# Output stage of a two-block kernel: three split weight buffers, a tile-by-tile end, and table loads behind the Silu

## The chip, the cores and the metric

The kernel runs as one program on one core of a Trainium2 chip. The metric is the device time of one execution in microseconds (us). Three runs of the kernel before gave 2280.24, 2282.44 and 2284.18 us, a median of 2282.44 us. The profile that is quoted below comes from another execution.

Engines carry the names of the profile: PE is TensorE (PEld its weight loads), DVE is VectorE, ACT is ScalarE, POOL is GpSimd, SP is SyncE, which here only issues DMAs.

## The reference

Two model blocks run one after the other over 512 tokens of width 1024, all in float32. The first is a gated mix of convolution and attention with a feed-forward part; the second holds an RWKV-7 mixer and then a latent attention (MLA) mixer. Only the end of the MLA mixer and what follows it is touched here:

```python
MLA_HEADS = 16; QK_NOPE = 128; QK_ROPE = 64; V_HEAD = 128      # D_INNER = 16 * 128 = 2048

def _rms_norm(x, g):
    y = xf * lax.rsqrt(jnp.mean(xf * xf, axis=-1, keepdims=True) + RMS_EPS)
    return (y * g).astype(x.dtype)

def _mla_mixer(x, pos, ...):
    h = x @ w_in                       # c_q, c_kv, k_rope and the gate input g
    ...
    o = _causal_block_attention(q_nope, q_rope, k_nope, k_rope, v).reshape(B, L, D_INNER)
    return (o * jax.nn.silu(g)) @ w_out            # [512, 2048] @ [2048, 1024]

h = h + _rms_norm(m, norm_post[i])
return h[:, N_META:]                   # the 16 meta tokens are dropped
```

## The kernel before

**Precision by three products.** A float32 product is made of three PE matmuls on parts rounded to a shorter format: high x high, high x low, low x high (`product`, L157 to L161). A weight block therefore has to be split before PE may use it: SP loads 512 KB or so into one of two `raw` buffers, and POOL writes the high part (L147) and then the low part (L150) into one of two buffers `w_hi`/`w_lo`. Such a block is a unit `u`; its buffers are those of slot `u % 2`. `split_ready` counts the splits, `unit_done` the units that PE has finished. POOL starts the split of unit `u` when unit `u - 2`, which used the same slot, is done.

**The head loop.** The 16 heads `h` run in the order written in the code, PE in `head_pe`, ACT in `head_act`, DVE in `head_dve`. A head has four query tiles `t`. For each tile PE computes scores, DVE takes the negative maximum `nmax`, ACT takes Exp (L2589), DVE normalises (reciprocal L2619, multiply L2622), PE transposes (`turn`, L2472 and L2474), DVE copies the result out (L2629, L2630), and after the four tiles PE makes the values product (L2489, L2491). DVE multiplies the result with the gate (L2605) and rounds it (`z2_hi`, L2607), POOL makes the low part (`z_low`, L2667). Between these steps PE does "fills" for the next heads, each written into a PSUM bank that must have been emptied first: `v0`, `v1`, `v2` (value weights, in even heads; banks 4, 5 and again 4), `rope` (in odd heads, bank 4), `gate` (bank 6), `ka`, `qn`, `kb` for the next head (banks 5, 4, 5). ACT empties the banks of all but the gate: `v_tok` (L2370, L2364), `q_sw` (L2356, four quarter copies), `kn_hi` (L2362), `qn_hi` (L2359). Head 13 has a shorter gate fill than the others; the rest of that gate is done in heads 13 and 14.

**Activation tables.** Exp and Silu are in different ACT tables. In heads 1 to 13 ACT does the Silu of gate `h + 1` right after the Exp of tile 1 (`gate_silu`, L2373 to L2376), and the Silu of gate 15 in head 14 just after the `ka` copy. The program gets an ACT_TABLE_LOAD ahead of the Silu (recorded at L2376) and one ahead of the next Exp (recorded at L2589).

**The output stage.** The 16 rows of blocks of `w_out`, `k` = 0 to 15, are the last 16 units. A "cell" is one token tile `t` (0 to 3) and one half of the 1024 output columns: three matmuls of 512 columns. A unit has eight cells, and all cells of the eight (tile, half) pairs accumulate in the eight PSUM banks (`OUT_BANK`). Unit 2 has a split buffer of its own, `out2_hi`/`out2_lo` (L2279 to L2287), which lies in memory that is free once gate 15 is done; units 0, 1 and 3 to 15 use the two slots. Units 0 and 1 and part of the stage's work are put into the last heads. POOL's order is: split 0, split 1, `z_low(14)`, split 2, `z_low(15)`, split 3 to 15. PE does units 2 to 13 with all cells, then unit 14 for tiles 0 and 1, then waits for unit 15's split and goes on tile by tile (L2566 to L2578).

**The end.** For each tile: ACT squares the 1024 columns and sums them (L2841), POOL adds epsilon (L2739) and takes the power -0.5 (L2741) into `fin_r`, DVE multiplies each half by `fin_r` and the norm weight `post_row` (L2936) and adds the residual `h_fin` (L2939), SP sends each half out (L2708).

Of the kernel before, what the change touches and what calls it, by code (L numbers as in the profile page):

```python
# [18 lines left out]
P = 128  # L19
# [51 lines left out]
def program(nc, io, out):  # L71
    with ExitStack() as base:
# [2058 lines left out]
        ssq, fin_r = put("ssq", [P, 2 * QB]), put("fin_r", [P, 2 * QB])  # L2131
# [147 lines left out]
        def split_out2(pool):  # L2279

            u = U_MO + 2
            pool.wait_ge(landed[u % 2], landings(u, u % 2))
            pool.wait_ge(unit_done, UNIT_AT["gate", MH - 1] + 1)
            nc.gpsimd.tensor_scalar(out2_hi[:], raw[u % 2][:, 0:D], 1.0, 0.0, ALU.mult, ALU.add).then_inc(split_hi, 1)
            pool.wait_ge(split_hi, u + 1)
            nc.gpsimd.tensor_tensor(out2_lo[:], raw[u % 2][:, 0:D], out2_hi[:].bitcast(F32), ALU.subtract).then_inc(split_ready, 1)
            pool.wait_ge(split_ready, u + 1)  # L2287
# [268 lines left out]
        def out_pe(pe):  # L2556
# [9 lines left out]
            for k in range(2, MH - 2):  # L2566
# [3 lines left out]
            pe.wait_ge(split_ready, U_MO + MH - 1)  # L2570
            pe.wait_ge(zl_ev, MH - 1)
# [98 lines left out]
        with nc.Block() as block:  # L2670
            @block.sync
            def _(sp):
# [30 lines left out]
                for k in range(2, MH):  # L2703
# [10 lines left out]
            def _(pool):  # L2714
# [259 lines left out]
```

## Time and profile before

| what | value |
|---|---|
| median of 3 runs | 2282.44 us (2280.24 to 2284.18) |
| the profiled execution's own time | 2284.97 us |
| its span | 2283.1 us |
| PE busy | 2235.6 us, 98% |
| DVE, ACT, POOL busy | 1237.7 us (54%), 831.5 us (36%), 1156.5 us (51%) |
| TensorE clock granted | 0.994 over the span |
| DMA queue of the program | 184.76 MB, 27.0% of 16 engines |

The profiled execution took 2.5 us more than the median; 1.9 us of its 2284.97 us lie outside its span. A line of the profile names the source line, the engine, the operation, the tiles written and read with partitions and elements, and how many were merged (x2). In brackets stands how long the engine sat idle before it and what released it. Matmul ends are modelled, so the distance between the starts of matmuls is the better measure of PE's pace.

### The profile page before, as it was taken

The numbers are of one execution on the slowest core, as the hardware profiler recorded it, in microseconds if no ns is written. First come the engines' busy times: TensorE is split into PE (matmuls) and PEld (weight loads), VectorE is DVE, ScalarE is ACT, GpSimd is POOL, SyncE is SP. The second block draws the span as 40 slices with busy tenths as digits, with TensorE's granted clock in tenths as the row PEclk, the third lists the DMA queues.
The fourth block names the chain that finished last, engine by engine and source line by source line (L and its number), as shares of the span: only waits on it lengthen the run. The fifth ranks groups of instructions, "written<-read, shape, count | busy, mean of one in ns | idle before, by whom it ended". The sixth has DMA issues, their size and how long they took to land.

```text
span 2283.1 us, 51404 instructions
## 1 busy us (share of the span) xinstructions
PE 2235.6 (98%) x21811; PEld 1805.1 (79%) x21811; DVE 1237.7 (54%) x2314; ACT 831.5 (36%) x1717; POOL 1156.5 (51%) x803
## 2 busy tenths in 40 slices
PE   8999999999999999999999999999998999999998
PEld 7778888788888677777777777777888878888876
DVE  4353357877831845555565566666531565555521
ACT  4122212333311445555555555554321343443300
POOL 4555567787765253444444444444546344343355
PEclk9999999999999999999999999999999999999999
DMA  3323323333332221222222222223323321221222
GB/s 115 83 75 84 83 87 92 95 97 97 104 102 97 71 63 60 69 80 83 73 69 78 69 69 69 71 75 128 130 66 106 106 74 47 58 63 42 76 96 92
DMA packets 262108, 188.04 MB, mean 82 GB/s; under 512 B 18283, under 2 KB 242409, under 8 KB 261497
## 3 DMA queue, kind: packets, MB, share of 16 engines
q1 hardware_dynamic: 261881, 184.76, 27.0%
q8 instruction: 174, 2.85, 0.5%
q14 instruction: 53, 0.43, 0.1%
HBM read 162.69 MB, written 22.04 MB: 81 GB/s over the span
## 4 chain that ended last, share of the span: by engine, by line
PE 90%; DVE 5%; POOL 2%; issue 1%; ACT 1%; SPq 0%; DMA 0%; POOLq 0%; DVEq 0%; ACTq 0%
PE ps L1353 19%; PE ps L159 16%; PE ps L160 15%; PE ps L161 15%; PE ps L1539 3%; PE ps L1555 3%; PE ps L1581 2%; PE ps L1528 2%; PE ps L1366 1%; PE ps L1495 1%; PE ps L2489 1%; PE ps L221 1%; PE ps L1467 1%; PE ps L1484 1%; PE ps L1517 1%
## 5 line engine op out<-in xcount | busy, mean ns | idle before, releaser
L150 POOL TENSOR_TENSOR w_lo<-raw,w_hi 128x1024 fp32r<-128x1024 f32 (+1 forms) x177 | 451.4, 2550 | 14.8
L147 POOL TENSOR_SCALAR w_hi<-raw 128x1024 fp32r<-128x1024 f32 (+1 forms) x177 | 195.4, 1104 | 480.6 <-PE ps L161 470.6
L159 PE MATMUL ps<-h_hi,w_hi 128*128 128x512 f32 x616 | 243.1, 395 | 1.8 <-DVE h_lo L1062 1.7
L161 PE MATMUL ps<-h_hi,w_lo 128*128 128x512 f32 x616 | 240.1, 390 | 0.0
L160 PE MATMUL ps<-h_lo,w_hi 128*128 128x512 f32 x616 | 239.7, 389 | 0.0
L1353 PE MATMUL ps<-mixed_k,raw 128*64 128x264 f32 x1024 | 149.3, 387 | 0.0
L1353 PE MATMUL ps<-mixed_r,raw 128*64 128x264 f32 x1024 | 143.9, 387 | 0.0
L1353 PE MATMUL ps<-mixed_g,raw 128*64 128x264 f32 x1024 | 138.2, 386 | 0.0
L159 PEld LDWEIGHTS ps<-h_hi,w_hi 128*128 128x128 f32 x616 | 115.8, 188 | 26.1 <-DVE h_lo L1062 2.8
L161 PEld LDWEIGHTS ps<-h_hi,w_lo 128*128 128x128 f32 x616 | 115.6, 188 | 24.4
L160 PEld LDWEIGHTS ps<-h_lo,w_hi 128*128 128x128 f32 x616 | 115.8, 188 | 23.2
L1353 PE MATMUL ps<-mixed_v,raw 128*64 128x264 f32 x1024 | 129.2, 389 | 2.4 <-DMA raw<-in_rwkv_w_in_dram 2.4
L1077 DVE SCALAR_TENSOR_TENSOR up_c<-up_raw,params,up_c 128x512 f32<-128x512 f32 x88 | 119.1, 1358 | 20.3 <-ACT up_c L832 18.7
L1881 DVE TENSOR_TENSOR x_m<-ps,lv_pad 128x640 f32<-128x640 f32 (+2 forms) x160 | 110.9, 726 | 9.7 <-PE ps L1539 5.2
L1945 POOL TENSOR_TENSOR kp<-k_b,kp 128x528 f32<-128x528 f32 x16 | 29.6, 1849 | 169.3 <-ACT kp L1674 169.3
L1539 PEld LDWEIGHTS ps<-t_m,mb 128*64 128x64 f32 x2752 | 96.1, 138 | 15.4 <-ACT mb L1662 3.4
L1353 PEld LDWEIGHTS ps<-mixed_v,raw 128*64 128x64 f32 x1024 | 69.6, 137 | 36.8 <-issue 5.4
L1539 PE MATMUL ps<-t_m,mb 128*64 128x64 f32 x2752 | 97.5, 222 | 0.2 <-DVE t_m L1887 0.2
L1962 POOL MEMSET uv<- 64x64 f32 x32 | 4.6, 145 | 178.8 <-PE ps L1510 177.9
L2589 ACT ACTIVATE xT<-ps,nmax 128x144 f32<-128x144 f32 (+1 forms) x64 | 34.4, 539 | 158.2 <-DVE nmax L2614 157.9
L1628 ACT ACTIVATE uv<-ps 64x64 f32<-64x64 f32 x128 | 27.9, 218 | 161.6 <-PE ps L1484 161.6
L1555 PEld LDWEIGHTS ps<-x_m,t_t 128*64 128x64 f32 x2240 | 77.8, 138 | 9.4 <-DVE x_m L1881 0.6
(462 smaller groups left out, 5959.3 us busy)
## 6 DMA issues: line engine op xcount, KB each, us to landing
raw<-in_rwkv_w_in_dram SPq DMA_DIRECT2D x64, 512.0 KB, 4.4
raw<-in_w_up_dram SPq DMA_DIRECT2D x44, 512.0 KB, 3.8
raw<-in_w_in_dram SPq DMA_DIRECT2D x41, 512.0 KB, 3.9
raw<-in_w_down_dram SPq DMA_DIRECT2D x22, 512.0 KB, 3.6
raw<-in_mla_w_in_dram SPq DMA_DIRECT2D x22, 512.0 KB, 4.0
sb_kept<-xT SPq DMA_DIRECT2D x16, 528.0 KB, 2.7
xT<-sb_kept SPq DMA_DIRECT2D x16, 528.0 KB, 4.7
raw<-in_rwkv_w_out_dram SPq DMA_DIRECT2D x16, 512.0 KB, 3.9
```

Source lines behind the costliest of these rows:

```text
L147: nc.gpsimd.tensor_scalar(w_hi[s][:, 0:width], raw[s][:, 0:width], 1.0, 0.0, ALU.mult, ALU.add).then_inc(split_hi, 1)
L150: nc.gpsimd.tensor_tensor(w_lo[s][:, 0:width], raw[s][:, 0:width], w_hi[s][:, 0:width].bitcast(F32), ALU.subtract).then_inc(split_ready, 1)
L159: nc.tensor.matmul(dst, w[0], x[0], start=start, stop=False)
L160: nc.tensor.matmul(dst, w[0], x[1], start=False, stop=False)
L161: return nc.tensor.matmul(dst, w[1], x[0], start=False, stop=stop)
L1077: nc.vector.scalar_tensor_tensor(out=up_c[:, ab, 1 + k, :], in0=up_raw[:, n % 4, 1 - k:1 - k + T1], scalar=prm(("cf1", "cf0")[k], n // 2 + ...
L1353: mm = nc.tensor.matmul(dst[m, :], raw_k[t % 2][:, k, m], mixed[t][:, k, cols], start=(k == 0), stop=(k == KD - 1))
L1528: mm = nc.tensor.matmul(ps[:, 2 + 3 * h + q, x * P:x * P + P], bk[own[h], c0 + x, :], rkv[own[h], c0 + x, 0:2 * C], start=True, stop=True)
L1539: mm = nc.tensor.matmul(ps[own[h], 2 + p, x * C:x * C + C], mb[:, c0 + x, own[h]], t_m[:, c0 + x, :], start=True, stop=True)
L1555: mm = nc.tensor.matmul(dst, t_t[:, c0 + x, :], x_m[:, c0 + x, h, :], start=True, stop=True)
L1581: mm = nc.tensor.matmul(ps[m, 6 + h, 0:T2 // 2], halves_ones[:, m], src(h), start=True, stop=True)
L1881: nc.vector.tensor_tensor(x_m[:, c0:c0 + m, :, :], part_of(2 + p, m).unsqueeze(2).to_broadcast([P, m, 2, C]), lv_pad[:, lv - 1, :, :].unsq ...
```

## The change

Five things are changed, all at the end of the second block.

1. **Three weight buffers.** Units 2, 5, 8, 11 and 14 of the output stage use the extra buffer, units 3, 6, 9, 12, 15 that of unit 0, units 4, 7, 10, 13 that of unit 1. The split of unit `k` (from 3 on) now waits until PE has finished unit `k - 3`, not `k - 2`. SP loads unit 2 ahead of `h_fin` and `post_row`.
2. **The split of unit 2** stands ahead of `z_low(14)` on POOL, where it stood behind it.
3. **Tile by tile.** PE does all cells only up to unit 12. Units 13 and 14 are done for tiles 0 and 1, then unit 15 for tile 0, then for tile 1; tiles 2 and 3 then get their cells of units 13, 14 and 15 one half after the other, with a signal after tile 2 and after each half of tile 3.
4. **The final norm.** DVE multiplies by `post_row` first, as soon as the square sum is there, and then does one operation with `fin_r` and `h_fin` per half. For tile 3 ACT squares the halves apart and takes the root itself by Ln and Exp(-0.5 x); POOL still adds epsilon to the first half's sum.
5. **Table loads.** After each Silu from gate 2 on, ACT loads the Exp table at once.

The diff, cut to its core:

```diff
+        def slot_of(u):
+            return u % 2
...
+        def out_buffer(k):
+            if k % 3 == 2:
+                return out2_hi, out2_lo
+            s = slot_of(U_MO + k % 3)
+            return w_hi[s][:, 0:D], w_lo[s][:, 0:D]
+        def split_out(pool, k):
+            u = U_MO + k
+            s, (hi, lo) = slot_of(u), out_buffer(k)
+            pool.wait_ge(landed[s], landings(u, s))
+            pool.wait_ge(unit_done, UNIT_AT["gate", MH - 1] + 1 if k == 2 else u - 2)
...
             act.wait_ge(gate_raw, g + 1)
             nc.scalar.activation(gate[:, g, :], gate[:, g, :], ACT.Silu).then_inc(gate_ev, 1)
+            if g > 1:
+                nc.scalar.preload_act_table_set(LOG_EXP)
...
-            for k in range(2, MH - 2):
+            for k in range(2, MH - 3):
                 pe.wait_ge(split_ready, U_MO + k + 1)
                 pe.wait_ge(zl_ev, k + 1)
                 out_cells(pe, k, ALL_CELLS).then_inc(unit_done, 1)
-            out_cells(pe, MH - 2, [(0, 0), (0, 1), (1, 0), (1, 1)])
+            for k in (MH - 3, MH - 2):
+                pe.wait_ge(split_ready, U_MO + k + 1)
+                pe.wait_ge(zl_ev, k + 1)
+                out_cells(pe, k, [(0, 0), (0, 1), (1, 0), (1, 1)])
             pe.wait_ge(split_ready, U_MO + MH)
             pe.wait_ge(zl_ev, MH)
-            for t in range(QB):
-                if t >= 2:
-                    out_cells(pe, MH - 2, [(t, 0), (t, 1)])
+            for t in range(2):
                 out_cells(pe, MH - 1, [(t, 0), (t, 1)]).then_inc(o_mm, 1)
+            for half in range(2):
+                for k in range(MH - 3, MH):
+                    mm = out_cells(pe, k, [(2, half)])
+            mm.then_inc(o_mm, 1)
+            for half in range(2):
+                for k in range(MH - 3, MH):
+                    mm = out_cells(pe, k, [(QB - 1, half)])
+                mm.then_inc(o_mm, 1)
...
                 for k in range(2):
                     load_out_rows(sp, k)
+                load_out_rows(sp, 2)
                 sp.wait_ge(unit_done, UNIT_AT["gate", MH - 1] + 1)
                 sp.wait_ge(s_h, 48)
                 sp.dma_start(h_fin[:], h_rows_kept).then_inc(s_h, 16)
                 sp.dma_start(post_row[:], io["norm_post_2"][1].partition_broadcast(P)).then_inc(s_h, 16)
-                for k in range(2, MH):
+                for k in range(3, MH):
                     load_out_rows(sp, k)
...
+                split_out(pool, 2)
                 z_low(pool, MH - 2)
-                split_out2(pool)
                 z_low(pool, MH - 1)
                 for k in range(3, MH):
-                    split_mla(pool, U_MO + k)
+                    split_out(pool, k)
...
+                t = QB - 1
+                for half in range(2):
+                    act.wait_ge(o_mm, QB + half)
+                    at = (t, 2 * QB)[half]
+                    nc.scalar.activation(squares[...512 columns...], ps[:, OUT_BANK[t] + half, :],
+                                         ACT.Square, scale=D ** -0.5, accum_out=ssq[:, at:at + 1]).then_inc(o_sq, 1)
+                act.wait_ge(o_eps, QB)
+                act.wait_ge(o_sq, QB + 1)
+                nc.scalar.activation(..., ACT.Ln, bias=ssq[:, QB + t:QB + t + 1]).then_inc(o_eps, 1)
+                act.wait_ge(o_eps, QB + 1)
+                nc.scalar.activation(fin_r[:, t:t + 1], ..., ACT.Exp, scale=-0.5).then_inc(o_r, 1)
...
                 for t in range(QB):
+                    for half in range(2):
+                        dve.wait_ge(o_sq, t + 1 + (half if t == QB - 1 else 0))
+                        nc.vector.tensor_tensor(o_tok[:, t, cols], ps[:, OUT_BANK[t] + half, :], post_row[:, cols],
+                                                ALU.mult).then_inc(o_step, 1)
                     dve.wait_ge(o_r, t + 1)
                     for half in range(2):
-                        nc.vector.scalar_tensor_tensor(out=o_tok[:, t, cols], in0=ps[:, OUT_BANK[t] + half, :], scalar=fin_r[:, t:t + 1],
-                                                       in1=post_row[:, cols], op0=ALU.mult, op1=ALU.mult).then_inc(o_step, 1)
                         dve.wait_ge(o_step, 2 * t + half + 1)
-                        nc.vector.tensor_tensor(o_tok[:, t, cols], o_tok[:, t, cols], h_fin[:, t, cols], ALU.add).then_inc(o_ev, 1)
+                        nc.vector.scalar_tensor_tensor(out=o_tok[:, t, cols], in0=o_tok[:, t, cols], scalar=fin_r[:, t:t + 1],
+                                                       in1=h_fin[:, t, cols], op0=ALU.mult, op1=ALU.add).then_inc(o_ev, 1)
```

The order of the instructions on ACT in an even head (head 12; the other even heads with a Silu, 2 to 10, read the same). Before, from the Silu (`gate`) over the copies of the value fills (`v_tok`) to the Exp of tile 2 (`xT` from 128x400):

```order
L2376 ACT_TABLE_LOAD
L2376 ACTIVATE gate<-gate 128x512 [waits gate_raw]
L2370 ACTIVATE v_tok<-ps 128x512 [waits oo_mm,up_mm]
L2370 ACTIVATE v_tok<-ps 128x512 [waits up_mm]
L2589 ACT_TABLE_LOAD [waits pt_mm]
L2589 ACTIVATE xT,psum_r<-ps,nmax 128x400 [waits sc_max]
```

And now:

```order
L2387 ACT_TABLE_LOAD
L2387 ACTIVATE gate<-gate 128x512 [waits gate_raw]
L2389 ACT_TABLE_LOAD
L2381 ACTIVATE v_tok<-ps 128x512 [waits oo_mm,up_mm]
L2381 ACTIVATE v_tok<-ps 128x512 [waits up_mm]
L2608 ACTIVATE xT,psum_r<-ps,nmax 128x400 [waits pt_mm,sc_max]
```

The second load moved from behind the two `v_tok` copies to ahead of them. The number of loads in the head is the same.

ACT in head 14 and at the start of head 15, where the Silu of gate 15 stands. Before:

```order
L2376 ACT_TABLE_LOAD
L2376 ACTIVATE gate<-gate 128x512 [waits gate_raw]
L2359 ACTIVATE qn_hi<-ps 128x512 [waits up_mm]
L2362 ACTIVATE kn_hi<-ps 128x264 [waits unit_done]
L2589 ACT_TABLE_LOAD [waits pt_mm]
L2589 ACTIVATE xT,psum_r<-ps,nmax 128x144 [waits sc_max]
```

And now:

```order
L2387 ACT_TABLE_LOAD
L2387 ACTIVATE gate<-gate 128x512 [waits gate_raw]
L2389 ACT_TABLE_LOAD
L2370 ACTIVATE qn_hi<-ps 128x512 [waits up_mm]
L2373 ACTIVATE kn_hi<-ps 128x264 [waits unit_done]
L2608 ACTIVATE xT,psum_r<-ps,nmax 128x144 [waits pt_mm,sc_max]
```

The load moved from ahead of head 15's first Exp to ahead of the copies `qn_hi` and `kn_hi` that head 15's scores are made of.

POOL around the split of unit 2 (`out_hi`, `out_lo`). Before:

```order
L147 TENSOR_SCALAR w_hi<-raw 128x1024 [waits unit_done,split_ready,landed1]
L150 TENSOR_TENSOR w_lo<-raw,w_hi 128x1024 [waits split_hi]
L2667 TENSOR_TENSOR z_lo<-xT,z_hi 128x512 [waits zh_ev,zt_ev,split_ready]
L2284 TENSOR_SCALAR out_hi<-raw 128x1024 [waits unit_done,landed0,zl_ev]
L2286 TENSOR_TENSOR out_lo<-raw,out_hi 128x1024 [waits split_hi]
L2667 TENSOR_TENSOR z_lo<-xT,z_hi 128x512 [waits zh_ev,zt_ev,split_ready]
```

And now:

```order
L150 TENSOR_SCALAR w_hi<-raw 128x1024 [waits unit_done,split_ready,landed1]
L153 TENSOR_TENSOR w_lo<-raw,w_hi 128x1024 [waits split_hi]
L2295 TENSOR_SCALAR out_hi<-raw 128x1024 [waits unit_done,landed0,split_ready]
L2297 TENSOR_TENSOR out_lo<-raw,out_hi 128x1024 [waits split_hi]
L2686 TENSOR_TENSOR z_lo<-xT,z_hi 128x512 [waits zh_ev,zt_ev,split_ready]
L2686 TENSOR_TENSOR z_lo<-xT,z_hi 128x512 [waits zh_ev,zt_ev,zl_ev]
```

The two operations of the split stand directly behind those of unit 1, and both `z_lo` operations behind them.

## Rows read from the trace of the kernel before

**Rows 1.** The page's chain that ended last, shares of the span by engine.

```profile
PE 90%; DVE 5%; POOL 2%; issue 1%; ACT 1%; SPq 0%; DMA 0%; POOLq 0%; DVEq 0%; ACTq 0%
```

**Rows 2.** Timeline of head 2: start, duration, engine, line, operation [idle before, releaser].

```profile
1901.68 0.63 ACT L2376 ACTIVATE gate<-gate 128x512 f32<-128x512 f32 x1
...
1902.22 1.07 ACT L2370 ACTIVATE v_tok<-ps 128x512 f32<-128x512 f32 x2
...
1902.69 0.23 PE L2452 MATMUL ps<-causal_b,ident_b 128*128 128x128 bf16 x1
...
1902.94 0.28 PE L159 MATMUL ps<-w_hi,ckv_hi 128*16 128x256 f32 x1
...
1903.30 1.28 ACT L2589 ACT_TABLE_LOAD   x1
```

**Rows 3.** Timeline of PE in head 0, the same place.

```profile
1859.60 0.23 PE L2452 MATMUL ps<-causal_b,ident_b 128*128 128x128 bf16 x1
1859.64 0.31 PE L159 MATMUL ps<-w_hi,ckv_hi 128*16 128x256 f32 x1
```

**Rows 4.** Timelines of ACT and PE in head 3.

```profile
1923.28 2.39 ACT L2356 ACTIVATE q_sw<-ps 32x512 f32<-32x512 f32 x4 [2.18 <-PE ps L161]
1925.69 1.28 ACT L2589 ACT_TABLE_LOAD   x1
1927.47 0.19 ACT L2589 ACTIVATION_READ_ACCUMULATOR xT<-ps,nmax 128x1 f32 x1
...
1927.46 0.31 PE L2474 MATMUL ps<-ident,xT 128*128 128x32 f32 x2
1927.72 0.39 PE L159 MATMUL ps<-kn_hi,qn_hi 128*128 128x264 f32 x1
```

**Rows 5.** Timeline of head 13, scores of tile 3 and the next low part.

```profile
2144.05 0.39 PE L159 MATMUL ps<-kn_hi,qn_hi 128*128 128x264 f32 x1 [1.33 <-ACT xT L2589]
...
2147.50 0.43 DVE L2395 TENSOR_TENSOR kn_lo<-ps,kn_hi 128x264 fp32r<-128x264 f32 x1 [0.60 <-ACT kn_hi L2362]
```

**Rows 6.** Timeline of head 14 behind the Silu of gate 15.

```profile
2169.47 0.58 ACT L2359 ACTIVATE qn_hi<-ps 128x512 fp32r<-128x512 f32 x1
...
2171.47 0.63 PE L2472 MATMUL ps<-ident,xT 128*128 128x128 f32 x4 [0.18 <-DVE xT L2630]
```

**Rows 7.** Timeline of heads 14 and 15 around the split of unit 2.

```profile
2171.45 2.37 POOL L150 TENSOR_TENSOR w_lo<-raw,w_hi 128x1024 fp32r<-128x1024 f32 x1
...
2176.84 0.43 DVE L2607 CAST z_hi<-xT 128x512 fp32r<-128x512 f32 x1
...
2179.99 2.55 DVE L2622 TENSOR_SCALAR xT<-xT,prec 128x272 f32<-128x272 f32 x1
2180.02 2.36 POOL L2286 TENSOR_TENSOR out_lo<-raw,out_hi 128x1024 fp32r<-128x1024 f32 x1
...
2182.60 0.44 PE L2472 MATMUL ps<-ident,xT 128*128 128x128 f32 x2 [1.90 <-DVE xT L2622]
```

**Rows 8.** DMA issues from 2120 us on: KB each, median us to landing.

```profile
raw<-in_mla_w_out_dram SPq DMA_DIRECT2D x16, 512.0 KB, 3.3
```

**Rows 9.** Timelines of POOL, PE, ACT and DVE at the end.

```profile
2261.91 1.05 POOL L147 TENSOR_SCALAR w_hi<-raw 128x1024 fp32r<-128x1024 f32 x1 [1.90 <-PE ps L161]
...
2265.47 0.50 PE L159 MATMUL ps<-w_hi,z_hi 128*128 128x512 f32 x1 [1.13 <-POOL w_lo L150]
...
2267.16 1.03 ACT L2841 ACTIVATE squares<-ps 128x1024 f32<-128x1024 f32 x1 [81.04 <-PE ps L161]
2268.08 0.19 ACT L2841 ACTIVATION_READ_ACCUMULATOR squares<-ps 128x1 f32 x1
...
2273.96 1.02 ACT L2841 ACTIVATE squares<-ps 128x1024 f32<-128x1024 f32 x1 [1.60 <-PE ps L161]
...
2269.44 0.75 DVE L2936 SCALAR_TENSOR_TENSOR o_tok<-ps,fin_r,post_row 128x512 f32<-128x512 f32 x1 [76.11 <-POOL fin_r L2741]
...
2279.94 0.69 DVE L2939 TENSOR_TENSOR o_tok<-o_tok,h_fin 128x512 f32<-128x512 f32 x1
```

More of the change, by code:

```diff
@@ L2130, in program @@
         nmax, psum_r, prec = put("nmax", [P, 2]), put("psum_r", [P, 2]), put("prec", [P, 2])
-        ssq, fin_r = put("ssq", [P, 2 * QB]), put("fin_r", [P, 2 * QB])
+        ssq, fin_r = put("ssq", [P, 2 * QB + 2]), put("fin_r", [P, 2 * QB])
         assert put.end <= 121, put.end
@@ L2277, in split_mla @@
             split_unit(pool, u, u % 2, width=1280 if wide else 1024)
[L2279 to L2284, printed above, removed]
+        def out_buffer(k):
[8 more added lines that the diff above has]
+            pool.wait_ge(unit_done, UNIT_AT["gate", MH - 1] + 1 if k == 2 else u - 2)
+            nc.gpsimd.tensor_scalar(hi[:], raw[s][:, 0:D], 1.0, 0.0, ALU.mult, ALU.add).then_inc(split_hi, 1)
             pool.wait_ge(split_hi, u + 1)
-            nc.gpsimd.tensor_tensor(out2_lo[:], raw[u % 2][:, 0:D], out2_hi[:].bitcast(F32), ALU.subtract).then_inc(split_ready, 1)
+            nc.gpsimd.tensor_tensor(lo[:], raw[s][:, 0:D], hi[:].bitcast(F32), ALU.subtract).then_inc(split_ready, 1)
             pool.wait_ge(split_ready, u + 1)
@@ L2495, in out_cells @@
         def out_cells(pe, k, cells):
-            s = (U_MO + k) % 2
+            hi, lo = out_buffer(k)
             for t, half in cells:
                 cols = slice(512 * half, 512 * half + 512)
-                w = (out2_hi[:, cols], out2_lo[:, cols]) if k == 2 else w_cols(s, 512 * half, 512)
                 mm = product(ps[:, OUT_BANK[t] + half, :], (z2_hi[:, k, P * t:P * t + P], z2_lo[:, k, P * t:P * t + P]),
-                             w, k == 0, k == MH - 1)
+                             (hi[:, cols], lo[:, cols]), k == 0, k == MH - 1)
             return mm
@@ L2739, in _ @@
                     nc.gpsimd.tensor_scalar(ssq[:, QB + t:QB + t + 1], ssq[:, t:t + 1], EPS, None, ALU.add).then_inc(o_eps, 1)
-                    pool.wait_ge(o_eps, t + 1)
-                    nc.gpsimd.tensor_tensor(fin_r[:, t:t + 1], ssq[:, QB + t:QB + t + 1], eps_col[:, 3:4], ALU.pow).then_inc(o_r, 1)
+                    if t < QB - 1:
+                        pool.wait_ge(o_eps, t + 1)
+                        nc.gpsimd.tensor_tensor(fin_r[:, t:t + 1], ssq[:, QB + t:QB + t + 1], eps_col[:, 3:4], ALU.pow).then_inc(o_r, 1)
             @block.tensor
@@ L2838, in _ @@
                     head_act(act, h)
-                for t in range(QB):
+                for t in range(QB - 1):
                     act.wait_ge(o_mm, t + 1)
@@ L2842, in _ @@
                                          ACT.Square, scale=D ** -0.5, accum_out=ssq[:, t:t + 1]).then_inc(o_sq, 1)
+                t = QB - 1
+                for half in range(2):
+                    act.wait_ge(o_mm, QB + half)
+                    at = (t, 2 * QB)[half]
+                    nc.scalar.activation(squares[:, t, 512 * half:512 * half + 512], ps[:, OUT_BANK[t] + half, :],
+                                         ACT.Square, scale=D ** -0.5, accum_out=ssq[:, at:at + 1]).then_inc(o_sq, 1)
+                act.wait_ge(o_eps, QB)
+                act.wait_ge(o_sq, QB + 1)
+                nc.scalar.activation(ssq[:, 2 * QB + 1:2 * QB + 2], ssq[:, 2 * QB:2 * QB + 1], ACT.Ln,
+                                     bias=ssq[:, QB + t:QB + t + 1]).then_inc(o_eps, 1)
+                act.wait_ge(o_eps, QB + 1)
+                nc.scalar.activation(fin_r[:, t:t + 1], ssq[:, 2 * QB + 1:2 * QB + 2], ACT.Exp, scale=-0.5).then_inc(o_r, 1)
             @block.vector
```

3 lines of the change are left out of this document (1 added, 2 removed).

## The prediction

> **What bounds the kernel now.** I read the page first: PE is busy 98% of the span, and 90% of the chain that ended last is PE [rows 1]. So until the last matmul a wait costs time only if PE waits for it, and a wait on PE costs its full length, since nothing behind it gives it back. Then the waits of PE and the timelines of the heads, one even and one odd head in full. The reader is to see there that PE hardly waits, but that in several places it goes on within 0.1 us of the end of an ACT or DVE operation. Such a place is tight: what delays that operation delays PE by the same amount. The end of the span is the exception: from the first `o_tok` operation at 2269.44 to the last at 2279.94 (its end 2280.63) the bound is DVE [rows 9].
>
> **Part 5, table loads, even heads with a Silu (2, 4, 6, 8, 10, 12).** In head 2 the Silu runs 1901.68 to 2.31, the copies of fills `v0` and `v1` start at 1902.22, overlapping its tail, and the table load follows at 1903.30 [rows 2]. PE's fill `v2` goes into the bank of `v0` and so waits for the first copy. PE issues it at 1902.94, 0.25 us behind the matmul before it, where in head 0, which has no Silu, the distance is 0.04 us [rows 3]. The first copy of 0.6 us ends at 1902.82, just ahead of 1902.94. So this place is tight, and the copy is what PE waits for. The change puts the load between Silu and copy: it can start at 1902.31 and takes 1.28 us (1.29 with its gap, as 1925.69 in [rows 4]), so the copy starts at 1903.61 and not 1902.22: 1.39 us later, and PE with it. The load that goes from behind the copies was hidden beside the gate fill. Six heads: 6 x 1.39 = **+8.3 us**. Bounds: 0, if the gap of 0.25 us is something else, and 8.3; I take 8.3, since rows 2 give the order of events to 0.1 us.
>
> The Trainium skill (ScalarE: Activation LUTs, "What ACT_TABLE_LOAD costs") counts about 2.66 us for each switch, a load of 1283 ns and a drain of 1380 ns. The rows agree with the first number and show no drain: the load starts 0.02 us behind the quarter copies' end at 2.39 us after 1923.28 [rows 4]. By the page's sum the even heads would lose some 16 us.
>
> **Odd heads.** There ACT is idle 2.18 us ahead of the four `q_sw` copies [rows 4], which covers a load of 1.29 us. The load it replaces stood between `q_sw` and the Exp of tile 2. That Exp ends at 1927.66, and PE starts the scores of tile 3 at 1927.72; PE's two matmuls before start at 1927.46 and are 0.31 us long together, so it could have gone on near 1927.58; with the shorter first step I take 0.14 us. Six heads (1, 3, ... 11): -0.8 us. In head 13 the gate fill in front is half as long and PE waits 1.33 us for the Exp [rows 5]. The load's 1.29 us go, but next the fill `kb` waits for DVE's `kn_lo` at 2147.50, which hangs on DVE's own queue (rope work) and moves by only 0.1 us; PE would reach it 0.15 us too early. Net **-1.1 us**. Odd heads together -1.9 us.
>
> **Head 14.** The Silu of gate 15 is followed by `qn_hi` at 2169.47; DVE's `qn_lo` and the copy of turn 2 come behind it in DVE's order, and PE's turn 3 at 2171.47 already waits 0.18 us for that copy [rows 6]. The load moves this chain by 1.39 us: **+1.4 us**. The load that goes stood ahead of head 15's first Exp; PE does not wait for that Exp directly, so nothing comes back.
>
> **Part 2, the split of unit 2.** In head 15 a DVE multiply of 128x272 takes 2.55 us: it starts 0.03 us before POOL's `out_lo` and ends 0.16 us behind it [rows 7]. PE's turn 1 waits 1.90 us for it. What the row shows is that DVE gets nothing done on two SBUF operands or in its fast form while such a POOL operation runs. The Trainium skill says the same (GPSIMD Reference, "Specifications": SBUF interfaces shared with VectorE, contention with instructions in a 2-port mode or with two SBUF inputs); it would have me expect the same stall wherever the split goes. The new place: unit 1's split ends at 2173.82 [rows 7], so unit 2's runs to about 2177.5. DVE has only PSUM reads there in the shifted head 14 (its rounding of `z2_hi`, at 2176.84 before, comes at 2178.2). The data must have landed by 2174: its load is issued at 2167.9 as before, takes 3.3 us [rows 8], and no longer queues behind `h_fin`. So **-1.9 us**. If `z2_hi` met the split, 0.4 us would come back.
>
> **Parts 1 and 3, PE at the end.** From the Square of tile 0 at 2267.16 to that of tile 3 at 2273.96 PE does 30 matmuls: 0.227 us each, 5.44 for a unit of 24 [rows 9]. Split 15 starts at 2261.91 when unit 13 is done, and PE waits 1.13 us for it at 2265.47. With three buffers it starts a unit earlier, at 2256.5, and the wait goes; with the slower restart I count 1.3 us. Matmuls number the same.
>
> **Parts 3 and 4, the tail.** Before: first Square at 2267.16, sum at 2268.27, POOL's epsilon and power, DVE at 2269.44, then 8 x (0.7 + 0.7) = 11.2 us of DVE. Now tile 0 is ready 14 cells (42 matmuls) before the end and not 10: its Square starts near 2263, tile 1's 2264.4, tile 2's 2268.5, the halves of tile 3 at 2270.6 and 2273.96 - 1.3 = 2272.7. DVE is then free of a backlog: per tile two multiplies and two final operations, about 0.6 to 0.7 each, 2.5 us, against tiles that come 4.1 and 2 us apart; tile 2 is done by 2272.2. The last half decides. Square of 512 columns: 1.11 us for 1024 [rows 9], so between 0.55 and 1.11, I take 0.77; sum at 2273.4; multiply from 2273.5, 0.6; Ln and Exp on one column lie beside it (two short ACT operations, bounded by the 0.19 of the accumulator read below and the 0.6 of a 512 copy above); two final operations, 1.4: DVE ends at 2275.5 (2275.2 to 2276.3). From DVE's end to the span's end is 2283.1 - 2280.63 = 2.47 us for the last store; the two last stores now come 0.7 us apart instead of 1.4, for which I leave 0.1. Span end 2278.0, that is **-5.1 us** with the 1.3 of PE in it (-4.3 to -5.4).
>
> **The sum.** +8.3 - 1.9 + 1.4 - 1.9 - 5.1 = +0.8 us on the profiled span of 2283.1, thus 2283.9. The median of the runs is 2282.44, so I predict 2283.2 us. The two sides are each about 9 us and nearly cancel.
>
> **The rivals.**
> - *The reload costs nothing in the even heads* (the gap of 0.25 us is not the copy, or PE makes the loss good later). For it: the page shows ACT busy only 36%, and the load is short. Against: rows 2 and 3, and PE without slack. Time: 2283.2 - 8.3 = 2274.9; half of it recovered gives 2279.
> - *The tail gives only PE's wait* (slower than before). Mechanism: DVE's final operation now reads `o_tok` and `h_fin`, both in SBUF, and waits for `fin_r`; if a POOL operation of the root or the new multiply in front pushes each tile past the next one, DVE stays the bound as before, with 11.2 us behind the first Square's successor. It decides if a tile's DVE work is over 4.1 us (I count 2.5). Then -5.1 becomes about -1.3, and the time 2287.0. Against: the old second operation also had two SBUF operands and took 0.69 [rows 9].
> - *The change does not do what it says in part 2*: the split meets DVE's rounding and `z_low` then sits in front of the first multiply; the 1.9 us come back, 2285.1.
> - *A switch of tables waits for a drain*. As a mechanism of this kernel: ACT would be held behind each load for as long again as the load lasts, which in six even heads and head 14 adds 7 x 1.3 = 9 us: 2292. Rows 4 speak against it. The Trainium skill's section named above has that rule; by the trace it does not hold.
>
> **How the numbers follow.** My sum 64%; reload free or largely made good 15%; tail only PE's wait 6%; part 2 void 12%; drain 3%. My sum's own error is about 1.5 us, and three runs spread over 4 us. The range 2278.0 to 2287.0 takes in my sum, part 2 void and the half-recovered case, and leaves out most of the first rival and the drain. This kernel tells a difference from none at about 0.2%, 4.6 us: faster is under 2277.9, slower above 2287.0. Faster: 15% x 0.8 and a rest of the sum's error, 0.14. Slower: 3% + half of 6% and a rest, 0.08. Same: 0.78.
>
> **What would show it.** Head 2 of the changed kernel: the first `v_tok` copy 1.4 us behind where it was, and PE idle about 1.4 us before the `v2` fill, six times. PE's wait in head 13 gone, the one before turn 3 of head 14 grown from 0.18 to 1.6. The 128x272 multiply of head 15 down to well under 1 us and PE's 1.90 us wait gone. No wait of PE for a split in the output stage; last matmul to span end 5.5 us, where it was 9. A PE that does not wait for `v0` in the even heads would make the prediction wrong by up to 8 us.

## The result, and the profile after

The changed kernel is slower. Median of 20 runs 2286.34 us (2283.94 to 2288.60); 20 runs of the kernel before beside them gave 2282.07 us. The ratio is 1.002 with a 95% interval of 1.0014 to 1.0026, so 3 to 6 us slower. Predicted were 2283.2 us, within 2278.0 to 2287.0, and no measurable difference. The time lies inside the range, but 3.5 us of it were not in my sum, and most of this part of the document is about them.

The two profiled executions hardly differ (span 2283.2 us now, 2283.1 before; own time 2284.88 and 2284.97). Read by that alone, the change costs nothing. The page shows the same picture as [rows 1], with DVE's share of the chain down from 5% to 4%:

```profile
PE 90%; DVE 4%; POOL 2%; ACT 2%; issue 1%; SPq 0%; DMA 0%; DVEq 0%; POOLq 0%; ACTq 0%
```

A profile of the whole is a poor ruler here, because the part ahead of the heads, which is the same code in all kernels, took 1857.3 to 1861.5 us in the 14 profiles I have. So I cut every profile in three: the front, up to the start of the Exp of tile 2 in head 0; the heads, from there to the start of the last Exp of head 15; the tail, to the end of the span.

| profile | front | heads | tail |
|---|---|---|---|
| before | 1860.5 | 324.9 | 97.8 |
| after | 1858.2 | 332.5 | 92.5 |
| after - before | -2.3 | +7.6 | -5.3 |

The front's -2.3 us does not come from the change: before had one more stretch at half TensorE clock there, in the same code. The touched parts cost +2.3 us, not 0.

**Even heads.** Timeline of head 2 after the change; it answers to [rows 2].

```profile
1899.27 0.63 ACT L2387 ACTIVATE gate<-gate 128x512 f32<-128x512 f32 x1
...
1899.92 1.28 ACT L2389 ACT_TABLE_LOAD   x1
...
1900.28 0.23 PE L2465 MATMUL ps<-causal_b,ident_b 128*128 128x128 bf16 x1
...
1901.22 1.09 ACT L2381 ACTIVATE v_tok<-ps 128x512 f32<-128x512 f32 x2
...
1901.96 0.28 PE L162 MATMUL ps<-w_hi,ckv_hi 128*16 128x256 f32 x1 [1.45 <-ACT v_tok L2381]
```

The load sits between Silu and `v_tok`; the copy begins 0.02 us behind it; PE stands idle for 1.45 us until the copy of `v0` has emptied the bank. The waits of PE over the heads (line waited for, us in total, times, longest):

```profile
PE ps L162 <- ACT v_tok L2381: 8.7, 6, 1.5
PE ps L2485 <- DVE xT L2641: 2.7, 7, 0.4
PE ps L2485 <- DVE xT L2649: 1.8, 2, 1.6
PE ps L162 <- DVE kn_lo L2408: 0.2, 1, 0.2
```

Six times 1.45 us for the copy, and no wait for it before. From tile 2 to tile 3 each of these heads is 1.37 to 1.42 us longer than before, except head 10 with 2.97.

**Head 10.** PE's timeline across its wait, then the same stretch by windows (us, busy time and count of PE, PEld, DVE, ACT and POOL, then granted clock, DMA share, GB/s).

```profile
2078.39 0.23 PE L2465 MATMUL ps<-causal_b,ident_b 128*128 128x128 bf16 x1
2080.07 0.28 PE L162 MATMUL ps<-w_hi,ckv_hi 128*16 128x256 f32 x1 [1.45 <-ACT v_tok L2381]
...
2081.20 0.63 PE L162 MATMUL ps<-u_hi,w_hi 128*128 128x512 f32 x1
2081.63 0.63 PE L163 MATMUL ps<-u_lo,w_hi 128*128 128x512 f32 x1
2082.06 0.63 PE L164 MATMUL ps<-u_hi,w_lo 128*128 128x512 f32 x1
...
2083.72 0.39 PE L162 MATMUL ps<-u_hi,w_hi 128*128 128x512 f32 x1
```

```profile
1960.00:2078.00 118.00, 113.82 (x674) 96.23 (x674) 68.84 (x162) 47.02 (x94) 50.37 (x29) 1.00 0.23 61
2078.00:2086.00 8.00, 6.55 (x30) 5.12 (x30) 1.34 (x5) 3.34 (x7) 0.17 (x1) 0.79 0.00 0
```

Before its wait PE runs at the full clock (2.4 GHz, 1.00 in the first window). Right behind the end of the wait it falls to the half (1.2 GHz): matmuls of 512 columns then start 0.43 us apart, and from 2083.72 on 0.23 us apart again. The clock record of this core has this stretch at 2080.2 us, 3.4 us long. It costs 2.97 - 1.40 = 1.6 us. The kernel before has a granted clock of 1.00 throughout the heads.

**Head 14**, answering to [rows 6]:

```profile
2175.61 1.28 ACT L2389 ACT_TABLE_LOAD   x1
...
2176.91 0.60 ACT L2370 ACTIVATE qn_hi<-ps 128x512 fp32r<-128x512 f32 x1
...
2178.93 0.63 PE L2485 MATMUL ps<-ident,xT 128*128 128x128 f32 x4 [1.59 <-DVE xT L2649]
```

PE's wait ahead of turn 3 has grown from 0.18 to 1.59 us.

**Split of unit 2**, answering to [rows 7]: both POOL operations end before DVE comes to them.

```profile
2177.49 2.35 POOL L153 TENSOR_TENSOR w_lo<-raw,w_hi 128x1024 fp32r<-128x1024 f32 x1
...
2181.07 2.35 POOL L2297 TENSOR_TENSOR out_lo<-raw,out_hi 128x1024 fp32r<-128x1024 f32 x1
...
2184.30 0.43 DVE L2626 CAST z_hi<-xT 128x512 fp32r<-128x512 f32 x1
...
2187.45 0.36 DVE L2641 TENSOR_SCALAR xT<-xT,prec 128x272 f32<-128x272 f32 x1
```

**The tail**, answering to [rows 9]. The halves of tile 3, Ln and Exp on ACT, the last matmul, and DVE's last two operations:

```profile
2275.86 0.60 ACT L2868 ACTIVATE squares<-ps 128x512 f32<-128x512 f32 x1 [0.93 <-PE ps L164]
...
2277.47 0.39 PE L164 MATMUL ps<-w_hi,z_lo 128*128 128x512 f32 x1
...
2277.90 0.60 ACT L2868 ACTIVATE squares<-ps 128x512 f32<-128x512 f32 x1 [1.35 <-PE ps L164]
...
2278.68 0.29 ACT L2872 ACTIVATE ssq<-ssq 128x1 f32<-128x1 f32 x1
2279.00 0.20 ACT L2875 ACTIVATE fin_r<-ssq 128x1 f32<-128x1 f32 x1
2279.24 1.41 DVE L2975 SCALAR_TENSOR_TENSOR o_tok<-o_tok,fin_r,h_fin 128x512 f32<-128x512 f32 x2
```

PE does not wait in the output stage, and from the start of the last matmul to the end of the span it is 5.7 us, where I had 5.5 and before it was 9.6.

### The profile page after: what moved, and what is told of

Same layout as the page of the kernel before. It is cut to its first block, busy times and chain, and to the rows that moved or that the text cites. A ratio compares the mean times of both kernels' runs of the same rounds, so it can differ in the third digit from the quotient of the medians.

```text
span 2283.2 us, 51399 instructions
## 1 busy us (share of the span) xinstructions
PE 2233.4 (98%) x21811; PEld 1802.9 (79%) x21811; DVE 1234.9 (54%) x2314; ACT 833.7 (37%) x1721; POOL 1157.7 (51%) x802
## 4 chain that ended last, share of the span: by engine, by line
PE 90%; DVE 4%; POOL 2%; ACT 2%; issue 1%; SPq 0%; DMA 0%; DVEq 0%; POOLq 0%; ACTq 0%
PE ps L1356 19%; PE ps L162 16%; PE ps L163 15%; PE ps L164 15%; PE ps L1542 3%; PE ps L1558 3%; PE ps L1584 2%; PE ps L1531 2%; PE ps L1369 1%; PE ps L1498 1%; PE ps L2502 1%; PE ps L224 1%; PE ps L1470 1%; PE ps L1487 1%; PE ps L1520 1%
## 5 line engine op out<-in xcount | busy, mean ns | idle before, releaser
L153 POOL TENSOR_TENSOR w_lo<-raw,w_hi 128x1024 fp32r<-128x1024 f32 (+1 forms) x164 | 420.4, 2563 | 13.7
L150 POOL TENSOR_SCALAR w_hi<-raw 128x1024 fp32r<-128x1024 f32 (+1 forms) x164 | 182.3, 1111 | 461.1 <-PE ps L164 451.0
```

The lines of the kernel that those rows point to most:

```text
L150: nc.gpsimd.tensor_scalar(w_hi[s][:, 0:width], raw[s][:, 0:width], 1.0, 0.0, ALU.mult, ALU.add).then_inc(split_hi, 1)
L153: nc.gpsimd.tensor_tensor(w_lo[s][:, 0:width], raw[s][:, 0:width], w_hi[s][:, 0:width].bitcast(F32), ALU.subtract).then_inc(split_ready, 1)
```

## The experiments

Times are medians. Each ratio is to the kernel before on the same chip, with its 95% interval. Heads and tail are cut from each kernel's profile as above. One run of this kernel varies with a standard deviation of 1.7 us, so the mean of 5 to 11 runs is good to 0.5 to 0.8 us, and the median a little less; the profile's segments agree with one another to 0.3 us where the code is the same.

| kernel | median (runs) | ratio | heads | tail | half-clock stretch in the heads |
|---|---|---|---|---|---|
| before | 2282.4 (92 in all) | | 324.9 | 97.8 | none |
| g2 before again | 2282.05 (11) | 0.9993 (0.9985 to 1.0002) | 324.6 | 97.8 | none |
| g1 part 2 alone | 2281.78 (11) | 0.9996 (0.9987 to 1.0005) | 323.2 | 97.8 | none |
| e1 no early load | 2275.53 (8) | 0.9972 (0.9962 to 0.9982) | 323.1 | 92.5 | none |
| e2 odd heads only | 2275.67 (9) | 0.9970 (0.9960 to 0.9980) | 321.3 | 92.5 | none |
| e7 split late | 2274.86 (7) | 0.9968 (0.9957 to 0.9980) | 320.9 | 92.5 | none |
| e8 old norm | 2277.81 (11) | 0.9980 (0.9971 to 0.9988) | 321.4 | 94.7 | none |
| f1 v0 first | 2274.88 (5) | 0.9961 (0.9949 to 0.9974) | 320.4 | 92.5 | none |
| f2 norm first | 2270.37 (5) | 0.9943 (0.9930 to 0.9955) | 316.5 | 92.5 | none |
| after | 2286.34 (20) | 1.0020 (1.0014 to 1.0026) | 332.5 | 92.5 | head 10, at 2080.2 |
| e3 loads alone | 2291.99 (5) | 1.0043 (1.0030 to 1.0056) | 332.5 | 97.8 | head 8, at 2035.3 |
| e4 wait filled | 2286.90 (11) | 1.0018 (1.0009 to 1.0026) | 332.6 | 92.5 | head 14, at 2180.0 |
| e5 even heads only | 2287.07 (11) | 1.0023 (1.0014 to 1.0032) | 333.4 | 92.5 | head 4, at 1946.5 |
| e6 gate 15 only | 2279.89 (11) | 0.9989 (0.9980 to 0.9998) | 324.0 | 92.5 | none |

### The early loads

**e1_no_preload.** In this and in e2, e5 to e8, f1 and f2 one load of the same table stands ahead of the last Squares, since the Ln and Exp at the end would otherwise each get a load of their own.

```diff
-            if g > 1:
-                nc.scalar.preload_act_table_set(LOG_EXP)
...
+                nc.scalar.preload_act_table_set(LOG_EXP)
                 for t in range(QB - 1):
                     act.wait_ge(o_mm, t + 1)
```

> The changed kernel without part 5 (no table load behind any Silu; one load of the same table ahead of the last Squares, where ScalarE is idle, so that the Ln and Exp at the end find it). By my sum the loads cost 6 x 1.4 + 1.4 and save 0.9 + 0.8, so the kernel becomes 8.1 us faster than the changed one: 2278.2 us, ratio to before 0.998. Clock theory: the PE waits of 1.45 us also make TensorE's clock fall to half once more per run, which costs 2 us more; then 2276 us, and no half-clock stretch in heads 2 to 14. Rival (the loads cost nothing by themselves, the 4.3 us come from the tail): 2286 us.

2275.53 us, 10.8 below the changed kernel, where the loads by my sum cost 8.1. Part 5 thus turns a gain of 7 us into a loss of 4. Of the rest of 2.7 us the heads of the two profiles show 1.2 to 1.3: 1.6 for the half-clock stretch that e1 does not have, less 0.4, since in e1 the rounding of `z2_hi` meets the split (see g1). What remains, some 1.4 us, lies in no part that the edit touches.

**e2_odd_heads.**

```diff
-            if g > 1:
+            if g > 1 and g % 2 == 0:
```

> The changed kernel with the early load only in the odd heads (gates 2, 4, ... 14), none in the even heads and none behind the Silu of gate 15; one load ahead of the last Squares. My sum: 6 x 1.4 + 1.4 = 9.8 us faster than the changed kernel: 2276.5 us; 1.7 us below e1. With the clock's part 2274.3 us. Rival (odd heads gain nothing): the same as e1.

The heads are 1.8 us shorter than in e1, as the sum has it (1.7). The medians do not show it (2275.67 and 2275.53). The difference of two such medians is good to about 0.8 us, so noise alone is a poor reason; e2's front was 0.8 us longer than e1's in the profiles, and the rest stays open.

**e3_preload_alone.**

```diff
+            if g > 1:
+                nc.scalar.preload_act_table_set(LOG_EXP)
```

> The kernel before with part 5 alone. My sum: +8.4 + 1.4 - 0.9 - 0.8 = +8.1 us: 2290.2 us (ratio 1.0036). Clock theory: 2 us more, 2292.4 us, and its mean clock lower than that of the kernel before. Rival (tail is to blame): 2282 us.

2291.99 us, 9.3 more than the 2282.67 of before beside it. The clock theory had the better number, for the wrong reason in part: the profile shows +8.1 us for the loads and 1.6 for a half-clock stretch, but also -2.1 us, since the collision of [rows 7] is gone although the split is where it was (see e7).

**e4_stall_filled.**

```diff
-                for c in ((0, 1), (2, 3), (4,))[int(kind[1])]:
+                for c in ((0, 1), (2, 3, 2, 3) if 0 < x < 7 else (2, 3), (4,))[int(kind[1])]:
```

> The changed kernel in which PE does the 12 matmuls of the fill v1 twice in heads 2, 4, ... 12 (1.3 us each time), so that the time in which it waits for the first v_tok copy is filled with work. If the cost is the length of the wait alone: as the changed kernel within 0.5 us, 2286.3 us. Clock theory (the idle 1.45 us bring down the clock): no wait at v2, no half-clock stretch in heads 2 to 14, 2284.1 us. If the PE wait were not set by the copy, the added work would come on top: 2294 us.

The clock theory's number (2284.1) is missed: 2286.90, near the 2286.3 of waits that cost their length alone. The time thus decides nothing for the clock; the profile says why. The wait was only half filled: six waits of 0.7 us remained, and the one of 1.6 us in head 14 was untouched.

```profile
PE ps L162 <- ACT v_tok L2381: 4.0, 6, 0.7
...
PE ps L2485 <- DVE xT L2649: 1.8, 2, 1.6
```

And it was at that one that the clock fell this time: PE goes on at 2179.26, and the stretch begins at 2180.0 (the window's granted clock is in the last columns).

```profile
2179.26 0.63 PE L2485 MATMUL ps<-ident,xT 128*128 128x128 f32 x4 [1.61 <-DVE xT L2649]
```

```profile
2179.00:2185.00 6.00, 5.74 (x25) 4.52 (x26) 1.98 (x6) 1.05 (x4) 4.58 (x3) 0.72 0.91 358
```

### Which wait, and which part of the tail

**e5_even_only** and **e6_gate15_only.**

```diff
-            if g > 1:
+            if g > 1 and g % 2 == 1 and g < MH - 1:      # e5
+            if g == MH - 1:                              # e6
```

> The changed kernel with the early table load only in the six even heads (gates 3, 5, ... 13); none in the odd heads, none behind the Silu of gate 15; one load ahead of the last Squares. Without any early load the time was 2275.5. Waits alone: 6 x 1.4 on top of 2275.5, 2283.9 us. Clock theory (an idle PE of 1.45 us brings on a half-clock stretch of 3.4 us, worth 1.6 us, in some heads): 2 to 3 us more, 2286.5 us, mean clock of the timed runs 0.994 where without any early load it was 0.996. Rival (the clock falls because of the wait in head 14 alone): 2283.9.

> The changed kernel with the early table load only behind the Silu of gate 15 in head 14; one load ahead of the last Squares. Waits alone: 1.4 us on top of 2275.5, 2276.9 us. Clock theory: the one wait of 1.6 us can bring on one half-clock stretch, at most 1.6 us: up to 2278.5 us. If the wait in head 14 alone is what lowers the clock, all of the 2.7 us: 2279.6.

e5 gave 2287.07 us, so the even heads alone bring all of the extra cost (11.5 us above e1 for 8.4 of waits), and head 14 is not needed for it. Its profile shows the stretch in head 4, behind the second of its waits:

```profile
1946.29 0.28 PE L162 MATMUL ps<-w_hi,ckv_hi 128*16 128x256 f32 x1 [1.45 <-ACT v_tok L2381]
```

```profile
1945.00:1951.00 6.00, 4.71 (x17) 3.73 (x18) 0.88 (x3) 2.57 (x6) 0.00 (x0) 0.72 0.00 0
```

e6 gave 2279.89 us, 4.4 above e1, where its heads are only 0.9 longer (1.4 for the wait, less 0.4 since the rounding of `z2_hi` no longer meets the split). Its profile has no stretch in the heads. Its front has 27.3 us at half clock where the others have 17.1 or 20.5, in code that is the same. The profiled execution took 2279.68 us, so it is a typical one, and of the 2.8 us by which its span is longer than e1's, 2.0 lie in that front. That a single wait of 1.6 us costs so much is therefore not shown; the median is unexplained by 1.9 us even with one stretch in every run, and why this kernel's front ran slower stays open.

**e7_split_late.** On top of e2.

```diff
-                split_out(pool, 2)
                 z_low(pool, MH - 2)
+                split_out(pool, 2)
```

> The kernel with early loads in the odd heads only (2275.7 us), with the split of unit 2 put back behind the low part of head 14. My step: DVE's multiply of 128x272 in head 15 again takes 2.55 us beside POOL's out_lo, PE waits 1.9 us again: 2277.6 us. Rival: in the kernel with the loads alone added to the kernel before, the wait was gone although the split stood where it was, so the place of the split may not matter: 2275.7 us.

No loss: 2274.86 us, and heads of 320.9 us, 0.4 shorter than with the split early. The multiply was not caught. In e7, and then in e3:

```profile
2178.12 0.36 DVE L2641 TENSOR_SCALAR xT<-xT,prec 128x272 f32<-128x272 f32 x1
2178.17 2.56 POOL L2297 TENSOR_TENSOR out_lo<-raw,out_hi 128x1024 fp32r<-128x1024 f32 x1
```

```profile
2186.99 0.36 DVE L2624 TENSOR_SCALAR xT<-xT,prec 128x272 f32<-128x272 f32 x1
2187.04 2.55 POOL L2286 TENSOR_TENSOR out_lo<-raw,out_hi 128x1024 fp32r<-128x1024 f32 x1
```

In [rows 7] DVE begins 0.03 us ahead of POOL and takes 2.55 us. Here it begins 0.05 us ahead, takes 0.36, and POOL takes 0.2 us longer. Between the lost and the won cases lie some 0.02 us.

**e8_old_norm.** Part 4 undone on top of e2; three buffers and tile order stay.

```diff
-  per tile: o_tok = ps * post_row (both halves);  o_tok = o_tok * fin_r + h_fin
+  per half: o_tok = ps * fin_r * post_row;        o_tok = o_tok + h_fin
-  tile 3: two Squares of 512 columns, Ln and Exp on ScalarE
+  tile 3: one Square of 1024 columns, power on POOL
```

> The kernel with early loads in the odd heads only (2275.7 us) with the old final norm (part 4 undone: ScalarE squares tile 3 whole, POOL takes the root of all four tiles, DVE multiplies by the root and the weight, then adds the residual); three buffers and the tile order stay. My step: for the last tile Square and sum 1.2 us, epsilon and power 1.0, four DVE operations 2.9, so 5.1 us behind the last matmul against 2.75 now: 2.3 us slower, 2278.0 us, and the tile order with the buffers keeps 2.8 of the 5.1 us. Rival (all of the tail's gain is the norm): 2279.5 us; rival (all of it is PE order and buffers): 2275.7.

2277.81 us against 2278.0 expected; the tail is 94.7 us against 92.5. So of the tail's 5.3 us, 2.2 are the norm and 3.1 the buffers and the tile order. The last tile in e8: Square, power, first and last operation of DVE.

```profile
2266.41 1.02 ACT L2863 ACTIVATE squares<-ps 128x1024 f32<-128x1024 f32 x1 [2.96 <-PE ps L164]
...
2267.92 0.57 POOL L2762 TENSOR_TENSOR fin_r<-ssq,eps_col 128x1 f32<-128x1 f32 x1
2268.52 0.75 DVE L2958 SCALAR_TENSOR_TENSOR o_tok<-ps,fin_r,post_row 128x512 f32<-128x512 f32 x1 [0.93 <-POOL fin_r L2762]
...
2270.70 0.69 DVE L2961 TENSOR_TENSOR o_tok<-o_tok,h_fin 128x512 f32<-128x512 f32 x1
```

### The collision, and a better version

**g1_part2_alone.** The load of unit 2 is also moved ahead of `h_fin`, as in the changed kernel.

```diff
+                split_out2(pool)
                 z_low(pool, MH - 2)
-                split_out2(pool)
```

> The kernel before with part 2 alone (split of unit 2 ahead of the low part of head 14, its load ahead of h_fin). My step: PE's wait of 1.9 us for the 128x272 multiply goes in every run, 2280.4 us. Rival (race theory): in the profiled run of before DVE's multiply and POOL's out_lo began within 0.03 us of each other and DVE lost; in two other kernels with the old order DVE won by 0.05 us and took 0.36 us. If the kernel before wins this race in most of its runs, part 2 is worth much less than 1.9 us on the median: 2281.5 to 2282.4, and the times of before are spread wider than those of this kernel.

**g2_before_again.** No edit.

> A second copy of the kernel before, unchanged. Ratio 1.000 within 0.001; what it differs by is the error of every comparison here. Its profile is a second look at the 128x272 multiply of head 15: 2.55 us if the collision is what this kernel always does, 0.36 us if it is a race that it wins in some runs (race theory). Half-clock stretches in heads 1 to 15: none (clock theory).

The profile of g1 has heads of 323.2 us, 1.4 to 1.7 less than the two profiles of before: +0.4 in DVE's rounding of `z2_hi`, which now meets the split (0.87 us in place of 0.43, the 0.4 that the prediction named for this case), and -2.1 in the multiply. The times show less of it: 2281.78 us against 2282.05 for the second copy of before and 2282.77 for the runs beside both; by the means g1 is 0.8 us faster than these 32 runs, uncertain by 0.5. The race theory's number was met and my step's (2280.4) missed, but the runs of before beside it were themselves 0.4 us above 2282.4, the interval of g1's ratio (0.9987 to 1.0005) still holds a gain of up to 3 us, and before is not spread much wider than g1 (1.7 and 1.4 us for the two sets of before, 1.5 for g1) as that theory also had it. So g1 decides between the two only weakly. The second copy lost the race in its profile too, again 0.03 us apart:

```profile
2179.39 2.55 DVE L2622 TENSOR_SCALAR xT<-xT,prec 128x272 f32<-128x272 f32 x1
2179.42 2.36 POOL L2286 TENSOR_TENSOR out_lo<-raw,out_hi 128x1024 fp32r<-128x1024 f32 x1
```

**f1_v0_first** and **f2_norm_first.** On top of e2, the copy of `v0` ahead of the Silu; and then, in the even heads, `normalise(0)` ahead of `gated`.

```diff
+                v0_first = t == 1 and h and h + AHEAD < MH and h % 2 == 0
+                if v0_first:
+                    fill_out(act, slots[0][0])
...
+            if h and h % 2 == 0:
+                normalise(0)
+                gated(dve, h - 1)
...
```

> The kernel with early loads in the odd heads only (2275.7 us), and in heads 2 to 12 with an even number the v0 copy ahead of the Silu and its table load. If PE's gap of 0.25 us at the v2 fill is the copy (my reading of rows 2 and 3), it shrinks to 0.04: 6 x 0.2 = 1.2 us faster, 2274.5 us. Rival (the gap is something else): 2275.7 us.

> As f1, and in the even heads DVE normalises tile 0 before it multiplies the value product with the gate, where it did it behind. PE waits 0.43 us for that normalisation in heads 2, 4, ... 14: if nothing else is late, 7 x 0.4 = 2.8 us faster, 2271.7 us. Rival (the low part or the next transposes wait in its place): 2274.5 us.

f1's heads are 0.9 us shorter than e2's, 0.12 to 0.17 in each of the six heads where 0.2 was expected, and in head 2 `v2` now starts 0.04 us behind the matmul before it: the gap of 0.25 us in [rows 2] was the copy. f2's heads are 3.9 us shorter again (expected 2.8): 0.65 in each of the six, where I had seven times 0.4. The waits below account for 2.6 us of it. At 2270.37 us f2 is 0.57% faster than before and 16 us faster than the changed kernel. PE's waits for the normalisation in e2 and in f2:

```profile
PE ps L2485 <- DVE xT L2641: 3.2, 7, 0.6
```

```profile
PE ps L2485 <- DVE xT L2644: 0.6, 1, 0.6
```

## Why the prediction was right, and what it missed

Each step, in the profiles. Where a place moved, the shift of the work around it is taken out.

| step | predicted | profile |
|---|---|---|
| even heads, 6 waits for `v_tok` | +8.3 | +8.4 |
| odd heads 1 to 11 | -0.8 | -0.9 |
| head 13 | -1.1 | -0.8 |
| head 14 | +1.4 | +1.4 |
| split of unit 2 | -1.9 | -2.1 |
| tail, with PE's 1.3 | -5.1 | -5.3 |
| sum | +0.8 | +0.7 |
| half-clock stretch in the heads | none | +1.6 |

**The even heads** went as read from rows 2 and 3: a place where PE goes on within 0.1 us of the end of a copy passes on every microsecond by which the copy is late. e1 and e5 bear it out: heads of 323.1 and 333.4 us, which is six times 1.43 and one stretch of 1.6. The rival that the reload costs nothing falls with the six rows of waits.

**The odd heads** came out in total, but the 0.15 us per head appears at the step to the next head, not between tiles 2 and 3 as I had it. Head 13 gave 0.8 instead of 1.1; the next wait is the one named, for `kn_lo`, 0.2 us.

**The tail**, in before's time (less the 5.35 us by which head 15's last Exp is later): first Square 2263.0 (I had 2263), last half 2272.6 (2272.7), DVE's end 2275.3 (2275.5), end of the span 2277.8 (2278.0). The rival that only PE's wait is gained falls with it and with e8.

**The drain at a table switch** is not there: in head 2 the copy starts 0.02 us behind the load's 1.28. The Trainium skill (ScalarE: Activation LUTs, "What ACT_TABLE_LOAD costs") has a drain of 1380 ns beside the load; no run here shows it, and by an estimate from its 2.66 us the even heads would have cost 16 us, twice what they do.

**What failed** are two things that are not sizes of a term.

First, I priced a wait of PE at its length (step "Part 5, even heads", and "a wait on PE costs its full length, since nothing behind it gives it back"). It costs more, since the clock can fall behind it. Of the five kernels with waits of 1.45 us or more behind an early load, four show exactly one stretch at half clock inside the heads, each beginning 0.2 to 0.7 us behind the end of such a wait; none of the nine others does. That these waits bring it on is shown by this coincidence and by e1 and e2 against e3 and e5. The length alone does not decide: before and its copy each have waits of 1.3 and 1.9 us in their heads, and e6 has its 1.3 and 1.6, without a stretch. Why one wait in seven does it, and which, is open: it was in heads 4, 8, 10 and 14.

Second, the step "Part 2, the split of unit 2" took a wait of 1.9 us from one profiled execution as what every run pays. Subtract heads and tail of a profile from the mean of the timed runs of the same kernel, and what is left should be the front (with what lies outside the span), the same for all. It is 1859.6 us for before (92 runs; 1859.0 to 1860.4 in its four sets) and 1859.3 for its second copy. For g1 it is 1860.8, for the changed kernel 1861.0, for e1 1860.3, and for eight of the nine others 1860.9 to 1861.7 (e6: 1863.0). So the timed runs of before are some 1.5 us faster than its profile says, a figure that its own sets move by 0.7 either way. The collision would explain it, if most timed runs win the race that both its profiles show lost, 0.03 us apart.

The fastest runs say more than the means. Take the shortest front of the 14 profiles (1857.3 us), add a kernel's own heads, tail and the 1.7 to 1.9 us outside the span, and no timed run should be much below that sum. In the twelve kernels other than before none of the 114 runs is more than 0.2 us below it. For before the sum is 2281.7 us, and 35 of the 103 runs of it and its copy are 0.5 to 2.2 us below it; with the 2.1 us of a race won the sum is 2279.6, and the fastest run took 2279.49. That speaks for the race, won in a third of the runs or more. It is still argued, not shown: a front with less half-clock time than any profile has would do the same, no timed run can be looked into, and no run here shifted the two operations against each other on purpose.

The same sum bears on the first error. For the four kernels with the stretch it includes the stretch, and none of their 47 timed runs is below it (the changed kernel: 2283.9, fastest run 2283.94), where runs without a stretch could be 1.6 us lower. So few timed runs, if any, seem to be without one. Their granted clock agrees: 0.994 or 0.995 in e5's runs, 0.996 in seven of e1's eight.

In means the changed kernel is 3.8 us slower (2285.97 - 2282.21): +0.7 for the steps, +1.6 for the stretch, and a remainder of 1.5 that the profiles' heads and tails do not hold. The first two are shown; the third is what is left over, so it agrees by construction, and the race is only the best account of it. By the medians it is 4.3.

The range held the time, but only just: its upper end was 2287.0. That is partly luck, since both errors went the same way and the forecast of no difference was off by 3.5 us. The profile before stood 2.5 us above the median; I noted it and gave no reason, and if the race is the cause, the second error lay there.

## What to carry to other kernels

Moving a table load ahead of work that frees a buffer costs the load's length if another engine is waiting for that buffer; put it where the engine is idle or behind the copies, and check each kind of iteration apart: the same line gained 1.8 us in the odd heads and lost 8.4 in the even ones. On a TensorE that is busy without a break, a new wait of 1.5 us costs its length and, at some of its occurrences, 1.6 us of halved clock. Before a wait seen in a profile is entered as a gain, look at what decided it: two operations that began 0.03 us apart are a race, and the timed runs may win it. Compare the fastest timed runs with what the profile's parts allow.

## What the runs showed of the hardware

- DVE's 128x272 multiply in SBUF and POOL's 128x1024 subtract do not run side by side, and the one that is a little ahead does not always win: with DVE 0.03 us ahead it waited to POOL's end (2.55 us, twice), with 0.05 us ahead it did not (0.36 us, twice) and POOL took 2.56 in place of 2.36. The Trainium skill (SBUF — State Buffer, "SBUF: two separate sides") says that of a DVE operation in a 2-port mode or with two SBUF inputs and a GpSimd operation, whichever starts first gets the shared ports for the whole instruction and the other fully blocks. The traces agree, except that in them a lead of 0.03 us is not enough. A small pair of the same kind stands in the heads of all 14 profiles: DVE's 128x144 multiply starts 0.06 us ahead of POOL's `z_lo`, and in all 203 cases it took 0.29 to 0.30 us; in head 0, with no `z_lo` beside it, it takes 0.29.
- The rounding of `z2_hi` (128x512, SBUF to SBUF) took 0.87 us in place of 0.43 beside POOL's `out_lo` in g1; it ended 0.28 us behind `out_lo`. I had counted it as a PSUM read that POOL does not touch. In the changed kernel it escapes, since head 14 is 1.4 us longer.
- Small POOL operations suffer beside DVE's final operation with two SBUF inputs: for tile 1 of the changed kernel epsilon on one column took 0.69 us in place of 0.22, the power 0.94 in place of 0.57.

```profile
2270.80 1.40 DVE L2975 SCALAR_TENSOR_TENSOR o_tok<-o_tok,fin_r,h_fin 128x512 f32<-128x512 f32 x2
...
2270.94 0.69 POOL L2759 TENSOR_SCALAR ssq<-ssq 128x1 f32<-128x1 f32 x1 [0.39 <-ACT squares L2862]
...
2271.71 0.94 POOL L2762 TENSOR_TENSOR fin_r<-ssq,eps_col 128x1 f32<-128x1 f32 x1
...
2275.02 0.22 POOL L2759 TENSOR_SCALAR ssq<-ssq 128x1 f32<-128x1 f32 x1 [2.37 <-ACT squares L2862]
...
2275.32 0.57 POOL L2762 TENSOR_TENSOR fin_r<-ssq,eps_col 128x1 f32<-128x1 f32 x1
```
